# Split weights kept in one region of four rows, with rows that advance by 64 bytes in the first block

## The chip, the cores and the metric

The kernel runs on one core of one Trainium2 chip. The metric is the time of one execution on the device in microseconds (us); lower is better.

## What is computed

Two blocks follow each other on 256 tokens of width 2048, all in float32. The first (16 meta tokens are put in front, so 272 columns) is a projection of the normed input, an attention with an indexer, a gated recurrence, sigmoid gates, a branch product and an output product. The second is a modulated projection, a neighbourhood attention, a Fourier mix, long convolutions, an output product and a gated feed-forward layer.

```python
def hybrid_layer(x, ...):                      # first block, 272 tokens
    h = rms_norm(x, norm_g)
    proj = h @ w_in                            # 2048 x 12368
    ...
    p = jnp.einsum('btnc,ncd->btnd', y, w_branch)
    g = jax.nn.sigmoid(gates.reshape(B, T, N_BRANCH, D))
    merged = jnp.sum(g * p, axis=2)
    return x + merged @ w_out
...
def second_block(x, c, ctx, ...):              # 256 tokens
    mod = (s_lat @ ada_w[l] + ada_b[l])[:, None, :]
    q, k, v, f, hy = split_projection(h @ w_in[l])
    ...
    x = x + g1 * (y @ w_out[l])
    x = x + g2 * conv_gated_mlp(modulate(rmsnorm(x, norm2_g[l]), sh2, sc2), *ffn)
    return rmsnorm(x, final_norm_g)
```

## The kernel before

Every weight matrix passes through the core once, in **chunks**. A chunk is four k tiles (rows of 128) by 256 output columns, 1024 float32 in each of the 128 partitions. Four chunks are a unit (256 output columns over the whole depth of 2048), and the units follow the list PHASES: in the first block FB, QB, IB, QI, K, KA, QA, VA, ZB, ZA, GA, GB (200 chunks), then E and F, and for the second block G, H, IH, IF, J, IQ, OA, OB, L, M0, M1; 668 chunks in all. START gives a phase's first chunk: IB 32, QI 48, K 64, QA 76, VA 92, ZB 100, E 196.

The product is made in float32r from a high and a low part of each operand. For chunk c ScalarE (ACT, `hi`) copies the loaded float32 chunk from a ring of four 1 MB buffers `raw` into a slot `whi`, VectorE (DVE, `lo`) writes the difference to a slot `wlo`, and TensorE (PE, `chunk`) does for each k tile six matmuls: high by high, low by high, high by low, each for two halves h of the output. In the phases of kinds Tall, Tx, K, BR, T and T8 the weights are the stationary operand (128 columns of a slot), and a row of an activation plane is the moving one: `phi` and `plo` in the first block (`r_hi` and `r_lo` in FB), `y`, `f`, `c`, `o`, `e` planes behind it. Tall and K read all 272 tokens, Tx reads 256 from token 16 on. In H and J (N2) and in M0 and M1 (DN) the activations are stationary and the weights move.

The sequencer engines run their lists in order. The list of each is written by slots: slot c of PE is chunk c and then what small products are due at c; slot c of ACT is `hi(c + 4)` and then its small work; slot c of DVE is `lo(c + 4)` and then its own. There are four slots of each part. `hi(c)` therefore waits until PE has done chunk c - 4 (semaphore `mm` at c - 3). Three chunks of E wait for chunk c - 3 as well, since from E on the slots lie 64 bytes further.

Where things lie (bytes in a partition): the slots follow each other from byte 34944, 4096 each, so k tile k4 of a slot is at 1024 * k4 in it; from E on all of it 64 further. `phi` begins 32768 behind the slots' start; its rows are 272 float32, 1088 bytes. The `f`, `y`, `c` and `o` planes have rows of 1024 bytes, `e` (the first six units of L) rows of 1056.

## Time and profile before

| | |
|---|---|
| median of 3 runs | 2171.58 us (2169.76 to 2172.3) |
| the profiled execution's span | 2171.5 us, first to last instruction |
| its own time outside the span | none is given apart; the span is 0.1 us below the median |
| PE, matmuls | busy 2132.8 us, 16496 records |
| DVE | busy 1464.8 us |
| ACT | busy 1037.6 us |
| granted TensorE clock, mean | 0.996 |
| DMA | 470.05 MB, mean 216 GB/s |

An engine's busy time is the union of its instructions' intervals. The mean of one matmul in a group is longer than its share of the busy time, since matmuls overlap in the pipeline: the pace is read from the distance of starts. A float32 instruction of the small products can leave two records.

### The profile page before, as it was taken

How to read it: one execution, taken by the hardware profiler on the slowest of the kernel's cores; microseconds unless marked ns; L12 is line 12 of the kernel's file. 1: busy time of each engine (PE TensorE's matmuls, PEld its weight loads, DVE VectorE, ACT ScalarE, POOL GpSimd, SP SyncE). 2: the span in 40 equal slices, each digit the busy share in tenths (PEclk: the TensorE clock that was granted, in tenths of full speed). 3: DMA queues.
4: the chain of work that ended last, by engine and by line, in shares of the span. 5: the costliest groups of instructions: out<-in, count | busy, mean ns of one | idle time of the engine just before them, and what ended most of it. 6: DMA issues, size and time to landing. Idle time of an engine off the chain costs nothing.

```text
span 2171.5 us, 38030 instructions
## 1 busy us (share of the span) xinstructions
PE 2132.8 (98%) x16496; PEld 1987.9 (92%) x16496; DVE 1464.8 (67%) x1850; ACT 1037.6 (48%) x1418; POOL 25.0 (1%) x47
## 2 busy tenths in 40 slices
PE   7999999999999999999999999999999999999998
PEld 7989999988999999998788999999999999988886
DVE  7666556666757698696665577789666665555665
ACT  6554334444454465454433455465444444444454
POOL 0000000110000000000000000000000000000000
PEclk9999999999999999999999999999999999999999
DMA  9765655775448878786565655766777775555553
GB/s 326 239 208 195 196 194 176 232 243 162 153 156 263 295 256 267 252 285 223 182 224 166 233 175 192 255 210 229 240 245 240 243 242 195 194 193 190 182 196 112
DMA packets 339156, 470.05 MB, mean 216 GB/s; under 512 B 14797, under 2 KB 312557, under 8 KB 326126
## 3 DMA queue, kind: packets, MB, share of 16 engines
q1 hardware_dynamic: 337838, 466.93, 64.5%
q8 instruction: 130, 2.13, 0.4%
q0 software_dynamic: 1152, 0.70, 0.1%
q14 instruction: 36, 0.29, 0.0%
HBM read 464.80 MB, written 2.10 MB: 215 GB/s over the span
## 4 chain that ended last, share of the span: by engine, by line
PE 91%; DVE 5%; ACT 2%; DMA 2%; issue 1%; SPq 0%; ACTq 0%; DVEq 0%
PE ps L1971 64%; PE ps L1982 11%; PE ps L1990 4%; DVE wlo L1191 2%; PE ps L2002 1%; PE ps L2060 1%; ACT whi L595 1%; DMA raw<-w_branch_dram 1%; PE ps L2321 1%; PE ps L2261 1%; PE ps L2223 1%; PE ps L2255 1%; DVE arena L1257 1%; DMA raw<-w_in_dram 1%; PE ps L1926 1%
## 5 line engine op out<-in xcount | busy, mean ns | idle before, releaser
L1191 DVE TENSOR_TENSOR wlo<-raw,whi 128x1024 fp32r<-128x1024 f32 (+1 forms) x668 | 814.6, 1221 | 661.7 <-ACT whi L595 658.5
L595 ACT ACTIVATE whi<-raw 128x1024 fp32r<-128x1024 f32 (+1 forms) x668 | 706.3, 1058 | 1065.2 <-PE ps L1971 860.5
L1971 PE MATMUL ps<-f_hi,whi 128*128 128x256 f32 x2112 | 422.0, 281 | 1.6 <-DVE f_lo L1835 1.6
L1971 PE MATMUL ps<-f_lo,whi 128*128 128x256 f32 x2112 | 413.8, 277 | 0.0
L1971 PE MATMUL ps<-f_hi,wlo 128*128 128x256 f32 x2112 | 413.5, 277 | 0.0
L1971 PEld LDWEIGHTS ps<-f_hi,whi 128*128 128x128 f32 x2112 | 320.7, 188 | 14.3 <-issue 11.8
L1971 PEld LDWEIGHTS ps<-f_hi,wlo 128*128 128x128 f32 x2112 | 319.9, 188 | 0.0
L1971 PEld LDWEIGHTS ps<-f_lo,whi 128*128 128x128 f32 x2112 | 319.9, 188 | 0.0
L1971 PE MATMUL ps<-phi,whi 128*128 128x256 f32 (+2 forms) x1440 | 300.7, 290 | 0.0
L1971 PE MATMUL ps<-plo,whi 128*128 128x256 f32 (+2 forms) x1440 | 288.4, 281 | 0.0
L1971 PE MATMUL ps<-phi,wlo 128*128 128x256 f32 (+2 forms) x1440 | 288.1, 281 | 0.0
L1971 PEld LDWEIGHTS ps<-phi,whi 128*128 128x128 f32 (+1 forms) x1440 | 219.7, 188 | 20.5 <-issue 18.2
L1971 PEld LDWEIGHTS ps<-phi,wlo 128*128 128x128 f32 (+1 forms) x1440 | 219.9, 187 | 0.5
L1971 PEld LDWEIGHTS ps<-plo,whi 128*128 128x128 f32 (+1 forms) x1440 | 219.4, 187 | 0.5
L1257 DVE SCALAR_TENSOR_TENSOR arena<-raw,cst,arena 128x1024 f32<-128x1024 f32 x120 | 153.5, 1279 | 2.8
L1982 PE MATMUL ps<-wlo,dhi 128*128 128x512 f32 x336 | 90.8, 392 | 0.0
L1982 PE MATMUL ps<-whi,dlo 128*128 128x512 f32 x336 | 90.6, 392 | 0.0
L1982 PE MATMUL ps<-whi,dhi 128*128 128x512 f32 x336 | 90.3, 391 | 0.0
L1982 PEld LDWEIGHTS ps<-whi,dlo 128*128 128x128 f32 x336 | 63.1, 188 | 14.1
L1982 PEld LDWEIGHTS ps<-whi,dhi 128*128 128x128 f32 x336 | 63.0, 188 | 13.8
L1982 PEld LDWEIGHTS ps<-wlo,dhi 128*128 128x128 f32 x336 | 63.1, 188 | 13.5
L1971 PE MATMUL ps<-y_hi,whi 128*128 128x256 f32 x256 | 50.9, 281 | 2.9 <-DVE wlo L1191 2.9
(380 smaller groups left out, 2595.1 us busy)
## 6 DMA issues: line engine op xcount, KB each, us to landing
raw<-w_in_dram SPq DMA_DIRECT2D x151, 1024.0 KB, 5.9
raw<-ada_w_dram SPq DMA_DIRECT2D x96, 1024.0 KB, 5.0
raw<-ffn_w_up_dram SPq DMA_DIRECT2D x88, 1024.0 KB, 5.0
raw<-ffn_w_down_dram SPq DMA_DIRECT2D x44, 1024.0 KB, 5.2
raw<-w_out_dram SPq DMA_DIRECT2D x32, 1024.0 KB, 5.7
raw<-w_branch_dram SPq DMA_DIRECT2D x16, 1024.0 KB, 6.1
arena<-xT_dram SPq DMA_DIRECT2D x4, 544.0 KB, 6.6
arena<-ctxT_dram SPq DMA_DIRECT2D x1, 2048.0 KB, 11.1
```

What stands on the lines that cost most here:

```text
L595: nc.scalar.activation(whi[slot_of(c)][:, 0:w], src, ACT.Copy).then_inc(S("split_hi"), 1)
L1191: v.tensor_tensor(wlo[slot_of(c)][:, 0:w], src, whi[slot_of(c)][:, 0:w].bitcast(F32), ALU.subtract).then_inc(S("split_lo"), 1)
L1257: t = v.scalar_tensor_tensor(total, x, by, R(ADA_SUM[n - 1][half], 1024), ALU.mult, ALU.add)
L1926: l = mm(ps[2 * t + nb][:, :], x[:, kd, 128 * t:128 * t + 128], wx[:, 512 * nb:512 * nb + 512], start=False, stop=last)
L1971: l = mm(ps[2 * p + h][0:m, b:b + tt.stop - tt.start], wx[:, k], x[:, xi, tt], start=first, stop=last)
L1982: l = mm(ps[(4 if name == "M0" else 0) + 2 * t + nb][:, :], x[:, kd, 128 * t:128 * t + 128], wx[:, 512 * nb:512 * nb + 512], start=first, ...
L1990: l = mm(ps[2 * p + t][:, 0:UC], x[:, kt, 128 * t:128 * t + 128], wx[:, k], start=first, stop=last)
L2002: l = mm(ps[7][32 * j:32 * j + 32, :], cst[:, n % 16, :], raw[e % RING][:, 512 * j:512 * j + 512], start=n % 16 == 0, stop=n % 16 == 15)
L2060: x = mm(ps[4 + g % 2][:, 128 * (h - h0):128 * (h - h0) + 128], kk, qq, start=True, stop=True)
L2223: l = mm(ps[4 + m % 2][:, :], kF[:, kt, 128 * m:128 * m + 128], hfil[:, kt + (2 if m >= 2 else 0), :], start=kt == 0, stop=kt == 1)
L2255: l = mm(ps[4 + 2 * m + b // 2][:, :], kF[:, kt, 128 * b:128 * b + 128], u_tok[:, kt, 0:512], start=kt == 0, stop=kt == 1)
L2261: l = mm(ps[4 + t][:, :], kG[:, k, 128 * t:128 * t + 128], Yt[:, k, :], start=k == 0, stop=k == 3)
```

## The change

The eight slots become one region of four rows, one for each k tile of a chunk. Each row holds the high parts of the four slots (256 float32 each) and then the low parts. There are three views of the region. `w_all` (IB, K, KA, VA) and `w_own` (FB, QB, QI, QA, ZB, ZA, GA, GB), 64 bytes further, have rows of 2064 float32, 8256 bytes, which is 8192 + 64; `w_even`, from E on, has rows of 8192 bytes and begins where `w_all` does. The region takes 64 float32 more than the slots did, and the 48 float32 of `gains` are put between it and `phi`, so that `phi` begins 33216 bytes behind the region's start; `small` shrinks from 128 to 120 and its parts are renumbered.

The chunks at which the view changes wait for chunk c - 3 where they waited for chunk c - 4: the first three of IB, QI, K, QA, VA and ZB, 18 chunks (`moved`), and those of E as before. The split's outputs are written as four pieces 8256 or 8192 bytes apart, a stationary operand is 128 columns of one row, and the moving operand of M0 and M1 is two pieces of 256 in place of 512 in one. The instructions of every engine and their order stay as they are.

```diff
-        whi = [sb(f"whi{i}", [128, CW], F32R) for i in range(4)]
-        wlo = [sb(f"wlo{i}", [128, CW], F32R) for i in range(4)]
-
-        whi += [at(f"whi{4 + i}", [128, CW], MEM + RING * RW + CW * i + 16, F32R) for i in range(4)]
-        wlo += [at(f"wlo{4 + i}", [128, CW], MEM + RING * RW + CW * (4 + i) + 16, F32R) for i in range(4)]
-
-        def slot_of(c):
-            return c % 4 + (4 if c >= START["E"] else 0)
+        wbase = top[0]
+        w_all = at("w_all", [128, 4, 2064], wbase, F32R)
+        w_own = at("w_own", [128, 4, 2064], wbase + 16, F32R)
+        w_even = at("w_even", [128, 4, 2048], wbase, F32R)
+        top[0] += 8256
+        gains = sb("gains", [128, 48])
+
+        def view_of(name):
+
+            if START[name] >= START["E"]:
+                return w_even
+            return w_all if name in ("IB", "K", "KA", "VA") else w_own
+
+        def weights(c, low):
+
+            s = 256 * (7 - c % 4 if low else c % 4)
+            return view_of(UNITS[CHUNK[c][0]][0])[:, :, s:s + 256]
...
-        small = sb("small", [128, 128])
+        small = sb("small", [128, 120])
         modL = sb("modL", [128, 96])
         modC = sb("modC", [128, 32])
-        gains = sb("gains", [128, 48])
...
-        rq, rqs = small[:, 108:124], small[:, 72:88]
-        shw = small[:, 124:126]
+        rq, rqs = small[:, 104:120], small[:, 72:88]
+        shw = small[:, 2:4]
...
+            names = [name for name, _, _ in PHASES]
+            moved = {START[b] + i for a, b in zip(names, names[1:]) if view_of(a) is not view_of(b) for i in range(3)}
...
-                    act.wait_ge(S("mm"), c - 2 if START["E"] <= c < START["E"] + 3 else c - 3)
-                nc.scalar.activation(whi[slot_of(c)][:, 0:w], src, ACT.Copy).then_inc(S("split_hi"), 1)
+                    act.wait_ge(S("mm"), c - 2 if c in moved else c - 3)
+                nc.scalar.activation(weights(c, False)[:, :, 0:w // 4], rx(src, 4), ACT.Copy).then_inc(S("split_hi"), 1)
...
-                v.tensor_tensor(wlo[slot_of(c)][:, 0:w], src, whi[slot_of(c)][:, 0:w].bitcast(F32), ALU.subtract).then_inc(S("split_lo"), 1)
+                n = w // 4
+                v.tensor_tensor(weights(c, True)[:, :, 0:n], rx(src, 4), weights(c, False)[:, :, 0:n].bitcast(F32), ALU.subtract)\
+                    .then_inc(S("split_lo"), 1)
...
-                                k = slice(n * k4 + 128 * h, n * k4 + 128 * h + m)
-                                l = mm(ps[2 * p + h][0:m, b:b + tt.stop - tt.start], wx[:, k], x[:, xi, tt], start=first, stop=last)
+                                l = mm(ps[2 * p + h][0:m, b:b + tt.stop - tt.start], wx[:, k4, 128 * h:128 * h + m], x[:, xi, tt], start=first, stop=last)
...
-                                       wx[:, 512 * nb:512 * nb + 512], start=first, stop=last)
+                                       wx[:, 2 * nb:2 * nb + 2, :], start=first, stop=last)
```

In the order of ACT's instructions around the first chunks of IB only the operand of the split changes; L824 is an exponential of the recurrence, L619 the evacuation of a unit of QB. Before:

```order
L595 ACTIVATE whi_55<-raw_49 128x1024 [waits mm,loaded0]
L824 ACT_TABLE_LOAD
L824 ACTIVATE arena<-arena 128x2048 [waits lv_diff]
L595 ACTIVATE whi_56<-raw_49 128x1024 [waits mm]
L619 ACTIVATE arena<-ps 128x256 [waits mm]
```

Now, with the `mm` of the first L609 one chunk further on:

```order
L609 ACTIVATE w_all<-raw_49 128x4x256 [waits mm,loaded0]
L838 ACT_TABLE_LOAD
L838 ACTIVATE arena<-arena 128x2048 [waits lv_diff]
L609 ACTIVATE w_all<-raw_49 128x4x256 [waits mm]
L633 ACTIVATE arena<-ps 128x256 [waits mm]
```

Nothing moved past anything else; what is queued behind the first split waits with it.

## Rows read from the trace of the kernel before

**Rows 1.** The page: busy time by engine; the chain that ended last, by engine.

```profile
PE 2132.8 (98%) x16496; PEld 1987.9 (92%) x16496; DVE 1464.8 (67%) x1850; ACT 1037.6 (48%) x1418; POOL 25.0 (1%) x47
...
PE 91%; DVE 5%; ACT 2%; DMA 2%; issue 1%; SPq 0%; ACTq 0%; DVEq 0%
```

**Rows 2.** The page's costliest groups: busy us, mean ns of one, idle before.

```profile
L1971 PE MATMUL ps<-f_hi,whi 128*128 128x256 f32 x2112 | 422.0, 281 | 1.6 <-DVE f_lo L1835 1.6
...
L1971 PE MATMUL ps<-phi,whi 128*128 128x256 f32 (+2 forms) x1440 | 300.7, 290 | 0.0
...
L1982 PE MATMUL ps<-whi,dhi 128*128 128x512 f32 x336 | 90.3, 391 | 0.0
```

**Rows 3.** Timeline of PE in E: start us, us, group of instructions.

```profile
722.11 0.39 PE L1971 MATMUL ps<-y_hi,whi 128*128 128x256 f32 x2
...
724.83 0.39 PE L1971 MATMUL ps<-y_hi,whi 128*128 128x256 f32 x2
```

**Rows 4.** Timeline of PE in GB, one chunk and the next one's start.

```profile
699.73 0.40 PE L1971 MATMUL ps<-phi,whi 128*128 128x256 f32 x2
...
701.14 0.40 PE L1971 MATMUL ps<-phi,whi 128*128 128x256 f32 x2
...
701.83 0.39 PE L1971 MATMUL ps<-phi,whi 128*128 128x256 f32 x2
...
702.54 0.28 PE L1971 MATMUL ps<-phi,whi 128*128 128x256 f32 x1
```

**Rows 5.** Timeline of PE in FB, one chunk and the next one's start.

```profile
57.37 0.41 PE L1971 MATMUL ps<-r_hi,whi 128*128 128x272 f32 x2
...
58.87 0.41 PE L1971 MATMUL ps<-r_hi,whi 128*128 128x272 f32 x2
...
59.61 0.42 PE L1971 MATMUL ps<-r_hi,whi 128*128 128x272 f32 x2
...
60.37 0.41 PE L1971 MATMUL ps<-r_hi,whi 128*128 128x272 f32 x2
```

**Rows 6.** Timeline of PE in IQ, one chunk and the next one's start.

```profile
1207.95 0.40 PE L1971 MATMUL ps<-f_hi,whi 128*128 128x256 f32 x2
...
1210.78 0.40 PE L1971 MATMUL ps<-f_hi,whi 128*128 128x256 f32 x2
```

**Rows 7.** Timeline of ACT ahead of the first matmul group of the recurrence.

```profile
113.63 1.07 ACT L595 ACTIVATE whi<-raw 128x1024 fp32r<-128x1024 f32 x1 [1.80 <-PE ps L1971]
...
116.01 1.91 ACT L824 ACTIVATE arena<-arena 128x2048 f32<-128x2048 f32 x1
117.83 1.04 ACT L595 ACTIVATE whi<-raw 128x1024 fp32r<-128x1024 f32 x1
118.77 0.64 ACT L619 ACTIVATE arena<-ps 128x256 f32<-128x256 f32 x2
120.63 1.06 ACT L595 ACTIVATE whi<-raw 128x1024 fp32r<-128x1024 f32 x1 [1.22 <-PE ps L1971]
```

**Rows 8.** Timeline of PE, the first matmul group of the recurrence.

```profile
129.45 1.16 PE L2060 MATMUL ps<-arena 128*128 128x128 f32 x8 [2.91 <-DVE arena L1453]
```

**Rows 9.** Timeline of ACT in slot 97, in VA.

```profile
388.91 1.06 ACT L595 ACTIVATE whi<-raw 128x1024 fp32r<-128x1024 f32 x1 [1.96 <-PE ps L1971]
389.88 0.25 ACT L778 ACTIVATE arena<-ps 16x128 f32<-16x128 f32 x1
390.03 0.36 ACT L779 ACTIVATE arena<-ps 128x256 f32<-128x256 f32 x1
390.30 0.42 ACT L852 ACTIVATE arena<-arena 128x272 f32<-128x272 f32 x1
```

**Rows 10.** Timeline of PE behind chunk 98, in VA.

```profile
392.05 0.62 PE L2109 MATMUL ps<-arena,mean 128*128 128x272 f32 x2
```

**Rows 11.** Groups of DVE between 100 and 300 us: busy us, mean ns.

```profile
L1191 DVE TENSOR_TENSOR wlo<-raw,whi 128x1024 fp32r<-128x1024 f32 x48 | 58.8, 1224 | 74.2 <-ACT whi L595 74.2
...
L1453 DVE TENSOR_TENSOR arena<-arena 128x1024 f32<-128x1024 f32 x7 | 8.5, 1219 | 0.0
```

More of the change, by code:

```diff
@@ L477, in _ @@
                                      (kz, A["k_z"]),
-                                     (small[0:64, 104:105], A["hy_b1_2"].rearrange("a q -> q a")),
-                                     (small[0:64, 105:106], A["hy_b2_2"].rearrange("a q -> q a")),
-                                     (small[0:64, 106:107], A["hy_freq_2"].rearrange("a q -> q a"))):
+                                     (small[0:64, 100:101], A["hy_b1_2"].rearrange("a q -> q a")),
+                                     (small[0:64, 101:102], A["hy_b2_2"].rearrange("a q -> q a")),
+                                     (small[0:64, 102:103], A["hy_freq_2"].rearrange("a q -> q a"))):
                         sp.dma_start(dst, src).then_inc(S("mlp_in"), 16)
@@ L1711, in filters @@
                         dve.wait_ge(S("fm_mm"), i + 1)
-                        chain(v.tensor_scalar(d, ps[4 + i][0:64, 0:256], small[0:64, 104 + i:105 + i], small[0:64, 106:107], ALU.add, ALU.mult))
+                        chain(v.tensor_scalar(d, ps[4 + i][0:64, 0:256], small[0:64, 100 + i:101 + i], small[0:64, 102:103], ALU.add, ALU.mult))
                         chain(v.tensor_scalar(n, d, 1 / (2 * np.pi), MAGIC, ALU.mult, ALU.add))
@@ L1922, in down_last @@
                 kd = 4 * (len(UNITS) % 2 ^ 1) + q
-                w = slot_of(CHUNKS - 4 + q)
-                for x, wx, last in ((dhi, whi[w], False), (dlo, whi[w], False), (dhi, wlo[w], q == 3)):
+                wh, wl = weights(CHUNKS - 4 + q, False), weights(CHUNKS - 4 + q, True)
+                for x, wx, last in ((dhi, wh, False), (dlo, wh, False), (dhi, wl, q == 3)):
                     for nb in range(2):
-                        l = mm(ps[2 * t + nb][:, :], x[:, kd, 128 * t:128 * t + 128], wx[:, 512 * nb:512 * nb + 512], start=False, stop=last)
+                        l = mm(ps[2 * t + nb][:, :], x[:, kd, 128 * t:128 * t + 128], wx[:, 2 * nb:2 * nb + 2, :], start=False, stop=last)
                 return l
@@ L1941, in chunk @@
                     pe.wait_ge(S(f"gemm_free{p}"), (u - p) // 2)
-                wh, wl = whi[slot_of(c)], wlo[slot_of(c)]
+                wh, wl = weights(c, False), weights(c, True)
                 xh, xl = {"E": (y_hi, y_lo), "G": (c_hi, c_lo), "H": (c_hi, c_lo)}.get(name, (phi, plo) if kind in ("Tall", "Tx", "K") else (f_hi, f_lo))
@@ L1953, in chunk @@
                     cc = {"Tall": slice(0, T), "Tx": slice(META, T), "K": slice(0, T)}.get(kind, slice(0, 258 if early else 256))
-                    n = 144 if kind == "K" else UC
                     b = 256 * (q // 2) if kind == "BR" else 0
@@ L1986, in chunk @@
                         kt = 4 * q + k4
-                        k = slice(UC * k4, UC * k4 + UC)
                         for x, wx, first, last in ((xh, wh, kt == 0, False), (xl, wh, False, False), (xh, wl, False, kt == KT - 1)):
                             for t in range(2):
-                                l = mm(ps[2 * p + t][:, 0:UC], x[:, kt, 128 * t:128 * t + 128], wx[:, k], start=first, stop=last)
+                                l = mm(ps[2 * p + t][:, 0:UC], x[:, kt, 128 * t:128 * t + 128], wx[:, k4, :], start=first, stop=last)
                 l.then_inc(S("mm"), 1)
```

## The prediction

> **What bounds the kernel now.** I read the page first. PE is busy for 98% of the span, DVE and ACT for 67% and 48%, and 91% of the chain that ended last lies on PE [rows 1]. So the time is PE's, and two things can change it: the pace of the matmuls, and stalls of PE where another engine is late. The costliest groups are those of the weights' product; none waits for more than 1.6 us in all [rows 2], so I went on to the pace, in the timeline.
>
> The mean of one matmul (281 to 290 ns) isn't the pace, since matmuls overlap. A chunk is 24 matmuls, and the distance from its first start to that of the next chunk is its price. In E it is 724.83 - 722.11 = 2.72 us, 113 ns a matmul [rows 3]. In GB, with the same 256 columns, 702.54 - 699.73 = 2.81 us, 117 ns [rows 4]. In FB, with 272 columns, 60.37 - 57.37 = 3.00 us, 125 ns [rows 5]. The granted clock is full in all three, and no wait stands in these rows. What differs is where the operands lie.
>
> **How they lie.** While PE streams the moving operand of one matmul, it loads the weights of the next. I take the distance from the weights of the next matmul to the moving operand, modulo 256 bytes; multiples of 256 (the halves h, the planes with rows of 1024, the chunk q of a unit, whose four plane rows advance by 4 * 64) drop out. In E, F, OB and the later L it is -64, that is 192, all the time: the slots lie 64 further there and everything else is a multiple of 256. In the first block the plane's row advances by 1088 bytes and the weights by 1024, so the distance is 64, 128, 192, 0 over the four k tiles of a chunk where 256 columns are read (first column 16, which is 64 bytes), and 0, 64, 128, 192 for IB, KA and VA. The chunk of GB shows it: its first two k tiles take 701.14 - 699.73 = 1.41 us, 0.705 each, the third, at 192, takes 0.69, and the fourth 0.71; in E every k tile takes 2.72 / 4 = 0.68 [rows 3, 4]. FB, which starts at 64 as well, has 0.75, 0.75, 0.74 and 0.76 [rows 5]. So the distance of 192 is the quickest, and even there the k tile isn't as quick as E's, since it comes out of one at another distance.
>
> But 192 isn't enough. IQ reads the same `f` planes at the same 192, and its chunk takes 1210.78 - 1207.95 = 2.83 us, 118 ns [rows 6]. So at a constant distance there are two paces, and a stretch keeps that in which it began.
>
> **The change, part by part.** (1) Distances. After the change `phi` is 33216 bytes behind the region, 192 modulo 256, and 64 + 64 cancel where `w_own` and a start at column 16 meet. FB's plane lies 109120 bytes behind `phi`, 64 modulo 256, which with 192 and less the 64 of `w_own` is again 192. Rows of weights and of planes both advance by 64. So five of the six matmuls of a k tile are at 192, throughout the first block. The sixth isn't: during it the weights of the next row are loaded, 64 further, while the moving row is still the old one, so that it stands at 128. From E on both shifted by amounts that leave 192 as it was: no change there, in distance.
>
> What is that worth? Bounds from rows. At best E's pace: 2.72 in place of 2.81 for each of the 144 chunks with 256 columns (QB, QI, QA, ZB, ZA 16 each, GA, GB 32 each), 13.0 us; for the 52 chunks with 272 (FB, IB 16 each, KA, VA 8 each, K 4) the same overhead over the columns, E's 113 ns scaled by 272/256 to 120 ns, 2.88 in place of 3.00, 6.2 us. Together 19 us. At worst IQ's pace: 0.02 more on 144 chunks, +2.9 us, and nothing on the others. I take neither end, as every k tile has its one matmul at 128 and so re-enters 192, which is what GB's third k tile does: 0.69 for each of the four, 2.76, 0.05 less than now. I count 0.04 a chunk, since a chunk that follows small products begins from yet another phase, as IQ's does: 144 * 0.04 = 5.8 us. For FB's kind 4 * 0.74 = 2.96, 0.04 * 52 = 2.1 us. Sum -7.9 us.
>
> (2) Waits. At six edges (IB, QI, K, QA, VA, ZB) three splits wait for one chunk more, 18 chunks. PE has the weights themselves early enough: at E's edge this wait exists, and PE goes through it without idling [rows 3]. The price is what stands behind the split, on ACT and DVE in order. Two places are tight.
>
> IB's edge: the split at 113.63 starts with the end of a chunk of QB; one chunk more (2.81) makes it 116.44. Behind it are a table load and the exponential, 116.01 - 113.63 = 2.38 later, the next split 1.82 after that, the evacuation 0.94 after that and 0.64 long: 116.44 + 2.38 + 1.82 + 0.94 + 0.64 = 122.22 for the third split, which now starts at 120.63 [rows 7]. All that follows, a second table load, a SiLU, a split and two DVE products, hangs on it up to the first matmul group of the recurrence, for which PE already waits 2.91 [rows 8]. So +1.6 us.
>
> ZB's edge: ACT's slot 97 is a split at 388.91, two copies and a square at 390.30, 1.39 later, 0.42 long [rows 9]. PE's norm product behind chunk 98 needs the square and starts at 392.05, when the chunk is through [rows 10]. The split now waits for that chunk's end: 392.1 + 1.39 + 0.42 = 393.9, so PE idles 1.9 us.
>
> At the four other edges what PE needs one slot later are short copies and masks. I take 0.3 each, 1.3 in all, an estimate; below is 0, above the larger of the two prices each, 7.6. Sum of (2): +4.8.
>
> (3) Shapes. DVE and ACT write four pieces. The nearest row is L1453, which writes runs with gaps: 1219 ns against the split's 1224 for as many elements [rows 11], so nothing; ACT and DVE have idle time besides. The moving operand of M0 and M1 is two pieces of 256. No row shows such an operand; now it is one of 512, in three groups of 336 matmuls [rows 2]. If the second piece cost as much as a step from E's pace to IQ's does for two matmuls of 256, 2 * (118 - 113) = 10 ns, it would be 1008 * 10 ns = 10.1 us; a gain is excluded, since the same columns are read. I take 0, nearer to the 3 ns by which L1453's gaps differ from the split's: the pieces lie a multiple of 256 apart, and nothing is loaded between them. `gains` and `small` only move.
>
> (4) Some of what the pace gains is lost again: PE waits 2.91 for ACT and DVE at the recurrence's start, and 1.9 at ZB's edge, whose chains begin two or three chunks before. That is about ten chunks of 0.04, 0.4 us; I count 0.6.
>
> Sum: -7.9 + 4.8 + 0.6 = -2.5. The profiled execution's span is 2171.5, and the median of the runs is 2171.58, so no correction: **2169.0 us**. What this measurement can tell from no change is 0.2%, 4.3 us.
>
> [...]
>
> **The rivals.**
> (A) The forecast: pace between, waits as priced. 2164 to 2173. Chance 0.42.
> (B) The quick pace locks in, as in E, in spite of the sixth matmul. For it: E enters 192 out of GB's drifting distances and is quick from its first chunk. Against it: GB's third k tile. -19.2 + 4.8, and some 2 us lost at the waits: 2159; with 256 columns alone quick, 2165. Chance 0.24. It ends under 2165.
> (C) The change doesn't do what it is built on: not the distance sets the pace (the other engines' writes do, or the two paces of IQ and F are chosen by something else), or the first block falls into IQ's pace. 2171.5 + 4.8 = 2176.3, with IQ's pace 2179. For it: 192 alone gave IQ nothing. Chance 0.22, slower. It decides once the pace gains less than 0.5 us in all, which is 3 ns a chunk over the 196.
> (D) The split moving operand of M0 and M1 costs PE 4 to 10 ns each: +4 to +10 on the forecast, 2173 to 2179. Nothing shows it. Chance 0.12.
>
> **How the numbers follow.** The predicted time is (A)'s. (B) reaches down to 2159, (C) up to 2179; leaving out the outer part of both, 2160 to 2178. Faster by over 0.2% (below 2167.2): (B) and a quarter of (A), 0.35. Slower (above 2175.9): most of (C) and half of (D), and a little for edges dearer than priced, 0.28. Within: 0.37.
>
> **What would show it.** A chunk of GB at 2.76 or 2.77 (2.72 under (B), 2.81 or more under (C)), one of FB at 2.96. The wait of PE ahead of the recurrence near 4.5 in place of 2.91, and a new one of 1.9 at the norm product behind chunk 98. M0 and M1 as long as before, and E, F and L at 2.72. The prediction is wrong if the first block has one pace from the first to the last chunk (then the sixth matmul does nothing), or if a phase from IQ's to OA's changes its own between 2.72 and 2.83, as these stretches keep the pace with which they begin and 32 chunks of IQ are worth 3.5 us.

## The result, and the profile after

The changed kernel takes 2179.04 us, the median of 4 runs (2176.48 to 2182.19); the kernel before took 2171.94 beside it (4 runs, 2169.76 to 2172.36). The ratio is 1.0034, with a 95% interval of 1.0019 to 1.0050: 7 us slower. 2169.0 was forecast, with 2160 to 2178 as the range. The profiled execution has a span of 2177.5 us, 6.0 above that of before, and a granted clock of 0.994 in place of 0.996. In every run whose span is on record the time is 1.8 to 2.0 us above the span, so the profiled execution of before took about 2173.4 us (an estimate: 2171.5 and 1.9), 1.4 above its median of 2171.94; the profiled one of the changed kernel took 2179.41, 0.4 above its own.

The page of the changed kernel, its busy times, the chain by engine, and three of the costliest groups, which answer to [rows 1, 2]:

```profile
PE 2136.5 (98%) x16496; PEld 1990.9 (91%) x16496; DVE 1464.5 (67%) x1850; ACT 1035.9 (48%) x1418; POOL 25.0 (1%) x47
...
PE 90%; DVE 5%; ACT 2%; DMA 1%; issue 1%; SPq 0%; ACTq 0%; DVEq 0%
...
L1985 PE MATMUL ps<-f_hi,w_even 128*128 128x256 f32 x4224 | 674.0, 280 | 2.5 <-DVE f_lo L1851 2.5
...
L1985 PE MATMUL ps<-phi,w_own 128*128 128x256 f32 x2304 | 385.9, 284 | 0.0
...
L1996 PE MATMUL ps<-w_even,dhi 128*128 128x512 f32 x672 | 167.6, 392 | 0.0
```

High and low parts are now one tensor, so a group that reads both has twice the count. The shares are as they were; a difference of 0.3% must be looked for by place. The length of a phase is the time from its first matmul to that of the next, and its pace the mean distance of starts inside its chunks, both worked out from the trace's starts (distances that other work interrupts left out):

| phase | before, us | ns | after, us | ns | difference |
|---|---|---|---|---|---|
| FB, QB | 105.22 | 125.0, 117.2 | 105.21 | 124.6, 117.0 | -0.01 |
| IB | 68.73 | 125.3 | 73.06 | 124.5 | +4.33 |
| QI, K, KA | 109.46 | | 110.60 | | +1.14 |
| QA | 67.47 | 117.3 | 67.34 | 117.0 | -0.13 |
| VA | 33.92 | 125.1 | 37.56 | 124.5 | +3.64 |
| ZB, ZA, GA, GB | 322.53 | | 322.42 | | -0.11 |
| E, F | 182.95 | 113.4 | 183.24 | 114.5, 113.4 | +0.29 |
| G | 47.63 | 115.9 | 46.33 | 113.4 | -1.30 |
| H | 45.23 | 117.8 | 43.52 | 113.4 | -1.71 |
| IH to OB | 430.26 | | 430.29 | | +0.03 |
| L | 494.49 | 114.3 | 494.49 | 114.3 | 0.00 |
| M0, M1 | 241.48 | | 241.48 | | 0.00 |

The loss is in IB and VA, where the two tight waits are (at the recurrence, and at the norm product ahead of ZB's edge), and the hoped-for gain of pace isn't in the table. PE's timeline in GB, one chunk in k tiles (start us, us, group):

```profile
703.83 0.40 PE L1985 MATMUL ps<-plo,w_own 128*128 128x256 f32 x2
...
704.54 0.39 PE L1985 MATMUL ps<-plo,w_own 128*128 128x256 f32 x2
...
705.23 0.40 PE L1985 MATMUL ps<-plo,w_own 128*128 128x256 f32 x2
...
705.94 0.39 PE L1985 MATMUL ps<-plo,w_own 128*128 128x256 f32 x2
...
706.63 0.40 PE L1985 MATMUL ps<-plo,w_own 128*128 128x256 f32 x2
```

and in FB, likewise, one chunk:

```profile
56.85 0.41 PE L1985 MATMUL ps<-r_lo,w_own 128*128 128x272 f32 x2
...
59.84 0.41 PE L1985 MATMUL ps<-r_lo,w_own 128*128 128x272 f32 x2
```

GB's chunk takes 2.80 us where it took 2.81 [rows 4], FB's 2.99 where it took 3.00 [rows 5]; 2.77 and 2.96 were forecast. The k tiles of GB alternate between 0.71 and 0.69.

The two waits of PE are as forecast. Of ACT ahead of the recurrence, then in slot 97, which answer to [rows 7, 9]:

```profile
116.35 1.06 ACT L609 ACTIVATE w_all<-raw 128x1024 fp32r<-128x1024 f32 x1 [1.80 <-PE ps L1985]
...
122.02 1.06 ACT L609 ACTIVATE w_all<-raw 128x1024 fp32r<-128x1024 f32 x1
...
397.43 1.06 ACT L609 ACTIVATE w_own<-raw 128x1024 fp32r<-128x1024 f32 x1 [1.83 <-PE ps L1985]
...
398.81 0.41 ACT L866 ACTIVATE arena<-arena 128x272 f32<-128x272 f32 x1
```

and of PE, which answer to [rows 8, 10], with the matmuls behind them:

```profile
130.83 2.08 PE L2073 MATMUL ps<-arena 128*128 128x128 f32 x8 [4.41 <-DVE arena L1469]
...
133.16 0.66 PE L1985 MATMUL ps<-plo,w_all 128*128 128x272 f32 x2
...
134.52 0.66 PE L1985 MATMUL ps<-plo,w_all 128*128 128x272 f32 x2
...
399.27 1.10 PE L2122 MATMUL ps<-arena,mean 128*128 128x272 f32 x2 [1.89 <-ACT arena L866]
```

The first split stands at 116.35 (116.44 was worked out), the third at 122.02 (122.22), and PE waits 4.41 us in place of 2.91; at the norm product it waits 1.89 us, where it didn't wait. But these rows show more: behind the first wait six matmuls of 272 columns take 134.52 - 133.16 = 1.36 us, 227 ns each in place of 125, and the same eight small matmuls 2.08 us in place of 1.16. The granted clock was at half there: the trace's record of the clock has 0.5 for 6.83 us from 129.8 us on. The table of PE by stretches (window, its length and PE's busy time, granted clock, DMA share, GB/s) for the kernel before:

```profile
126.00:138.00 12.00, 9.09 (x73) 1.00 0.48 141
370.00:384.00 14.00, 14.00 (x102) 0.88 0.53 178
396.00:404.00 8.00, 8.00 (x70) 1.00 0.56 188
740.00:748.00 8.00, 5.08 (x35) 0.85 1.07 371
```

and for the changed one:

```profile
126.00:138.00 12.00, 7.59 (x40) 0.72 0.60 205
370.00:384.00 14.00, 14.00 (x109) 0.94 0.78 260
396.00:404.00 8.00, 6.12 (x35) 0.79 0.40 120
```

At the recurrence and at the norm product the full clock has become 0.72 and 0.79. In 126 to 138 the fall counts (1.00 - 0.72) * 12 = 3.4 us of work at full speed, in 396 to 404 it counts (1.00 - 0.79) * 8 = 1.7. By the same record such a fall is a stretch of 3.41 us at half, so each counts 1.7 at most; behind the first wait two follow each other. No step of the prediction has this.

### The profile page after: what moved, and what is told of

The parts are those of the page before. It is cut to its first block, busy times and chain, and to the rows that moved or that the text cites. A ratio compares the mean times of both kernels' runs of the same rounds, so it can differ in the third digit from the quotient of the medians.

```text
span 2177.5 us, 38030 instructions
## 1 busy us (share of the span) xinstructions
PE 2136.5 (98%) x16496; PEld 1990.9 (91%) x16496; DVE 1464.5 (67%) x1850; ACT 1035.9 (48%) x1418; POOL 25.0 (1%) x47
## 4 chain that ended last, share of the span: by engine, by line
PE 90%; DVE 5%; ACT 2%; DMA 1%; issue 1%; SPq 0%; ACTq 0%; DVEq 0%
PE ps L1985 63%; PE ps L1996 11%; PE ps L2003 4%; DVE w_even L1206 2%; PE ps L2073 1%; PE ps L2015 1%; ACT w_even L609 1%; DMA raw<-w_branch_dram 1%; DVE arena L1273 1%; PE ps L2334 1%; PE ps L2274 1%; PE ps L2236 1%; PE ps L2268 1%; DMA raw<-w_in_dram 1%; PE ps L1942 1%
## 5 line engine op out<-in xcount | busy, mean ns | idle before, releaser
L1206 DVE TENSOR_TENSOR w_even<-raw,w_even 128x1024 fp32r<-128x1024 f32 x472 | 577.1, 1224 | 427.2 <-ACT w_even L609 424.5
L609 ACT ACTIVATE w_even<-raw 128x1024 fp32r<-128x1024 f32 x472 | 499.8, 1060 | 693.8 <-PE ps L1985 496.6
L1985 PE MATMUL ps<-f_hi,w_even 128*128 128x256 f32 x4224 | 674.0, 280 | 2.5 <-DVE f_lo L1851 2.5
L1985 PEld LDWEIGHTS ps<-f_hi,w_even 128*128 128x128 f32 x4224 | 567.4, 189 | 15.5 <-issue 10.9
L1985 PE MATMUL ps<-f_lo,w_even 128*128 128x256 f32 x2112 | 414.7, 278 | 0.0
L1985 PE MATMUL ps<-phi,w_own 128*128 128x256 f32 x2304 | 385.9, 284 | 0.0
L1985 PEld LDWEIGHTS ps<-phi,w_own 128*128 128x128 f32 x2304 | 316.6, 189 | 15.6 <-issue 14.8
L1985 PEld LDWEIGHTS ps<-f_lo,w_even 128*128 128x128 f32 x2112 | 320.0, 189 | 0.0
L1206 DVE TENSOR_TENSOR w_own<-raw,w_own 128x1024 fp32r<-128x1024 f32 x160 | 195.3, 1224 | 182.5 <-ACT w_own L609 181.7
L609 ACT ACTIVATE w_own<-raw 128x1024 fp32r<-128x1024 f32 x160 | 169.2, 1058 | 285.5 <-PE ps L1985 283.6
L1985 PE MATMUL ps<-plo,w_own 128*128 128x256 f32 x1152 | 228.5, 280 | 0.0
L609 ACT ACTIVATE w_all<-raw 128x1024 fp32r<-128x1024 f32 (+1 forms) x36 | 36.2, 1014 | 83.1 <-PE ps L1985 83.1
```

What stands on the lines that cost most here:

```text
L609: nc.scalar.activation(weights(c, False)[:, :, 0:w // 4], rx(src, 4), ACT.Copy).then_inc(S("split_hi"), 1)
L1206: v.tensor_tensor(weights(c, True)[:, :, 0:n], rx(src, 4), weights(c, False)[:, :, 0:n].bitcast(F32), ALU.subtract)\
L1985: l = mm(ps[2 * p + h][0:m, b:b + tt.stop - tt.start], wx[:, k4, 128 * h:128 * h + m], x[:, xi, tt], start=first, stop=last)
```

## The experiments

Theory 1: the loss is that of the six edges, idle time and half a clock behind it; and the distance of addresses does set the pace, but a row that advances with its planes keeps one matmul in six at another distance, and that is enough to hold the pace back. Against it stand that the layout itself costs, that the distance is of no account, and that the half clock has nothing to do with the waits. The kernel before ran beside all of them, with medians of 2171.54 to 2173.26.

**The waits alone.** The old slots, with the later wait at the six edges:

```diff
-                    act.wait_ge(S("mm"), c - 2 if START["E"] <= c < START["E"] + 3 else c - 3)
+                    act.wait_ge(S("mm"), c - 2 if any(START[b] <= c < START[b] + 3 for b in ('IB', 'QI', 'K', 'QA', 'VA', 'ZB', 'E')) else c - 3)
```

> The kernel before with its old slots, where the first three splits of IB, QI, K, QA, VA and ZB wait for one chunk more, as in the changed kernel. Theory 1, the waits and the lower clock behind the two stalls of PE made the loss: 1.6 us more of waiting at the recurrence's first group, 1.9 at VA's norm product, about 1.1 at the other edges, and 3.4 and 1.7 us for the clock at half behind them; 2179 to 2183. Theory 2, the new layout made the loss (strided writes of the splits, the two-piece operand, the pace): the waits alone cost the 4.8 us of the prediction or less, 2172 to 2177, with no stretch of lower clock behind them.

2180.27 us (8 runs), ratio 1.0033 (1.0022 to 1.0045), the same as the whole change. IB is 4.62 longer than before and VA 3.75, QI, K and KA 1.0 together. Its PE:

```profile
131.59 2.08 PE L2060 MATMUL ps<-arena 128*128 128x128 f32 x8 [4.38 <-DVE arena L1453]
...
400.36 1.13 PE L2109 MATMUL ps<-arena,mean 128*128 128x272 f32 x2 [1.89 <-ACT arena L852]
```

**The layout alone.** All of the first block through `w_own`, which needs no edge but E's; IB, K, KA and VA then stand at 128:

```diff
-            return w_all if name in ("IB", "K", "KA", "VA") else w_own
+            return w_own
```

> The changed kernel with w_own for all of the first block, so that no view changes before E and no split waits longer; IB, K, KA and VA are read at a distance of 128 instead of 192. Theory 1: the loss goes, and with 272 columns at 124.5 ns and G and H at whichever of the two paces they fall into it takes 2167 to 2173. Theory 2: it stays at 2177 to 2181.

2174.28 us (10 runs), ratio 1.0008 (0.9997 to 1.0018). IB is 70.51 and VA 34.08, so without the waits the loss is gone, and the new region, the four-piece writes and the two-piece operand cost nothing that these runs can measure: the interval reaches to 4 us, but in the profile L, M0 and M1 are as long as before to 0.02 us. IB, KA and VA at 128 run at 125.9 ns where the changed kernel has 124.5 and the drifting distance of before 125.2.

**The wait kept, PE kept busy.** 14 small matmuls whose result nobody reads, ahead of the wait at the recurrence; in the second kernel 7 more ahead of that at the norm product:

```diff
+                    if l == 0 and g == 0:
+                        for _ in range(14):
+                            mm(ps[4][:, 0:128], mean1[:, :], ident[:, :], start=True, stop=True)
...
-                    pe.wait_ge(S("nk_sq"), c + 1)
                     if c >= 1:
                         pe.wait_ge(S("nk_root"), c)
+                    if c == 3:
+                        for _ in range(7):
+                            mm(ps[4][:, 0:128], mean1[:, :], ident[:, :], start=True, stop=True)
+                    pe.wait_ge(S("nk_sq"), c + 1)
```

> The changed kernel with 14 extra products of 128x128 float32 on PE (into a bank that is written next; their result is not used) ahead of its wait for the recurrence's first group, so that PE is busy for about 3 of the 4.4 us. Theory 1, with the lower clock as a result of PE's idling: the granted clock stays at full behind it, and 3.4 us come back, 2174 to 2177. Rival: the clock falls anyway (it comes with time, not with idling), and the time stays at 2177 to 2181.

> The changed kernel, waits and all, with 14 small matmuls without use ahead of PE's wait at the start of the recurrence (as in the run before with these alone) and 7 more ahead of its new wait at the norm product behind chunk 98 in VA. Nothing of the reference is left out. Theory 1 (the added waits cost twice: as idle time, and because the granted clock halves behind them): at the norm product PE stays busy through the 1.9 us, the stretch of half clock at 396 is gone, and VA is 1.5 us shorter than in the run with the first filling alone for an equal number of such stretches around 375; the whole 1.5 to 2 us under that run, so about 2174 to 2175, a ratio of 1.001 to the kernel before, where the changed kernel has 1.0034. Rival (the stretches fall where they do for another reason, and filling one moves it to the next): the stretch of 396 stays or comes back within the next 30 us, and the whole stays at 2176 to 2179.

With the first filling: 2176.43 us (10 runs), ratio 1.0016 (1.0007 to 1.0026). With both: 2174.98 us (11 runs), 1.0017 (1.0007 to 1.0026). The second's PE at the norm product, and its stretches:

```profile
396.03 1.72 PE L2126 MATMUL ps<-ident,mean 128*128 128x128 f32 x14
398.08 0.72 PE L2128 MATMUL ps<-arena,mean 128*128 128x272 f32 x2 [0.33 <-ACT arena L866]
```

```profile
126.00:138.00 12.00, 10.72 (x90) 1.00 0.60 204
370.00:384.00 14.00, 14.00 (x92) 0.77 0.77 254
396.00:404.00 8.00, 7.67 (x62) 1.00 0.44 135
```

What each wait is for is as in the changed kernel (the norm product's two waits have changed places, so that the filling stands between them), and the norm product starts 2.3 us behind the last pair of its chunk in both; what differs is that PE has work. The clock is full at both places. IB falls from 73.06 to 70.39 with the first filling and stays (70.41); VA goes from 39.16 to 37.60 with the second. So the half clock at these two places hangs on PE's idling. Both predictions of Theory 1 hold for their places. But the second row, 370 to 384, also shows what I can't steer: a stretch of half clock that is in the kernel before too (0.88 in that window). No wait of PE stands ahead of it. What stands there, in the kernel before, is 3.6 us of matmuls of one column:

```profile
372.49 3.62 PE L2179 MATMUL ps<-mean,arena 128*128 128x1 f32 x32
```

So PE's idling is one thing that the half clock comes behind, and not the only one. In both filled kernels this stretch is twice as long and takes back 1.5 us in the profile. Of the four profiles of kernels with a filling (two more follow below) three have it twice as long; of the ten without, nine have it once and one not at all. Whether a filling brings that about isn't shown. The second filling is worth 1.56 us in VA, but against the kernel before beside them the two kernels have the same ratio, 1.0016 and 1.0017, so the times don't show it. That the fillings act rests on IB and VA in the profiles.

**What distance is worth.** Four kernels change the layout from E on, where the kernel before stands at 192 and the rows of weights and planes advance alike. The first three are the kernel before with its late slots moved (16 to 0, 32 and 48 float32: distances 0, 128 and 64); the fourth is the changed kernel with `w_all` from E on, so that the weights' rows advance by 64 and the planes' don't:

```diff
-        whi += [at(f"whi{4 + i}", [128, CW], MEM + RING * RW + CW * i + 16, F32R) for i in range(4)]
-        wlo += [at(f"wlo{4 + i}", [128, CW], MEM + RING * RW + CW * (4 + i) + 16, F32R) for i in range(4)]
+        whi += [at(f"whi{4 + i}", [128, CW], MEM + RING * RW + CW * i + 0, F32R) for i in range(4)]
+        wlo += [at(f"wlo{4 + i}", [128, CW], MEM + RING * RW + CW * (4 + i) + 0, F32R) for i in range(4)]
...
             if START[name] >= START["E"]:
-                return w_even
+                return w_all
```

> The kernel before with the slots from E on not moved by 64 bytes, so that the distance from the next weights to the moving rows is 0 instead of 192, constant, in all phases whose weights are stationary. Theory 1 (the distance sets the pace): a chunk of L takes clearly more than 2.72 us, about the 2.83 of the drifting kernels, some 20 us or more in all. Theory 2 (a constant distance is enough, whichever it is): 2.72 us stay, 2170 to 2176 in all.

> As late_0, with the slots moved by 128 bytes from E on: a constant distance of 128, which is that of the sixth matmul of each k tile in the changed kernel's first block. Theory 1: slower than 2.72 us a chunk in L, and if this distance is the worst, more than 2.83, so that one matmul in six at it costs what the other five gain. Theory 2: 2.72 us.

> The kernel before with the late slots (from E on) 128 bytes further, so that from E on the next weights stand at a constant distance of 64 modulo 256 from the moving operand, where the kernel before has 192, and earlier runs had 0 (120.0 ns a matmul in L) and 128 (118.9). Theory 1 (the distance sets a pace of its own at each of four values, and 192 alone is quick): L at 118 to 120 ns a matmul, L about 18 to 22 us longer than 494.5, E to L alike, the whole about 2205 to 2211. Rival (only the distances 0 and 128 are slow, and the pace before is that of every other place): L stays at 113.3, and the whole within 5 us of 2172. For M0 and M1, whose weights move and whose activations are loaded, the distance becomes 192 by Theory 1's reckoning, and their 241.5 us shift by a few us in either direction.

> The changed kernel with the rows of 8256 bytes (w_all) from E on too, over planes with rows of 1024 bytes, so that the distance there goes through 192, 128, 64, 0 in each chunk. If the distance sets the pace as before it seemed to in GB, a chunk of F and of L takes 2.80 to 2.83 us in place of 2.72, some 15 to 20 us in all over 300 chunks. If what matters is something else that first and second block differ in (the planes' rows of 1088 bytes, the other engines' work), it stays at 2.72.

One run each: 2210.90, 2206.34, 2185.44 and 2210.35 us, where the runs of the kernel before beside all experiments range from 2168.77 to 2178.09. PE's timeline for distance 0, one chunk of L, and then 16 matmuls of M0 and M1:

```profile
1604.51 0.40 PE L1971 MATMUL ps<-f_hi,whi 128*128 128x256 f32 x2
...
1607.39 0.40 PE L1971 MATMUL ps<-f_hi,whi 128*128 128x256 f32 x2
...
2049.64 1.07 PE L1982 MATMUL ps<-whi,dhi 128*128 128x512 f32 x4
...
2053.26 1.07 PE L1982 MATMUL ps<-whi,dlo 128*128 128x512 f32 x4
```

for distance 128:

```profile
1597.83 0.40 PE L1971 MATMUL ps<-f_hi,whi 128*128 128x256 f32 x2
...
1600.68 0.40 PE L1971 MATMUL ps<-f_hi,whi 128*128 128x256 f32 x2
```

for distance 64, in E and in L:

```profile
722.33 0.40 PE L1971 MATMUL ps<-y_hi,whi 128*128 128x256 f32 x2
...
725.16 0.40 PE L1971 MATMUL ps<-y_hi,whi 128*128 128x256 f32 x2
...
1585.46 0.39 PE L1971 MATMUL ps<-f_hi,whi 128*128 128x256 f32 x2
...
1588.18 0.39 PE L1971 MATMUL ps<-f_hi,whi 128*128 128x256 f32 x2
```

and of the kernel before, 16 matmuls of M0 and M1:

```profile
2049.94 1.08 PE L1982 MATMUL ps<-whi,dlo 128*128 128x512 f32 x4
...
2053.61 0.62 PE L1982 MATMUL ps<-wlo,dhi 128*128 128x512 f32 x2
```

| distance | ns a matmul (L) | a chunk, us | L against before, us |
|---|---|---|---|
| 192 (before) | 113.3 or 117.8 | 2.72 or 2.83 | 0 |
| 64 | 113.3 or 117.8 | 2.72 or 2.83 | +4.6 |
| 128 | 118.9 | 2.85 | +18.6 |
| 0 | 120.0 | 2.88 | +23.5 |
| 192, 128, 64, 0 in turn | 118.0 | 2.83 | +16.5 |

The distance sets the pace; that is settled by kernels that differ in one number. It isn't the address of the weights alone: from E on the changed kernel has them, modulo 256 bytes, where the kernel at distance 0 has them, with the planes 64 bytes lower, and its L takes 494.49 us where the other's takes 518.01. I had expected 64 to be slow: it is the equal of 192, and each of them has two paces. 128 has two as well: L runs at 118.9, the greater part of IQ at 120.0. In E and F the kernel at 64 is in the slow one and in L for the most part in the quick one, at the same addresses within each phase.

**One matmul in six.** The undisturbed part of L read with the changed kernel's first-block addresses: the activations of its later units are put into `phi` and `plo`, whose rows are 1088 bytes, and read through `w_own`. Second, the kernel before with only its low slots moved on by 64 bytes, so that two loads of six stand at 128 and nothing advances:

```diff
-            if START[name] >= START["E"]:
+            if START[name] >= START["E"] and name != "L":
                 return w_even
...
+                rows = name == "L" and not early
+                if rows:
+                    xh, xl = phi, plo
```

```diff
-        wlo += [at(f"wlo{4 + i}", [128, CW], MEM + RING * RW + CW * (4 + i) + 16, F32R) for i in range(4)]
+        wlo += [at(f"wlo{4 + i}", [128, CW], MEM + RING * RW + CW * (4 + i) + 32, F32R) for i in range(4)]
```

> The changed kernel where L from its seventh unit on keeps its activations in phi and plo (rows of 1088 bytes) and reads its weights through w_own (rows of 8256 bytes): the first block's new addresses, in a phase that is quick and undisturbed. If one matmul in six at 128 is what undoes the gain, L's chunks take 2.80 us as GB's do, some 12 us more in all over 152 chunks. If the first block is slow for another reason (the other engines' work there), L stays at 2.72 and the time at 2176 to 2182.

> The kernel before with only the late low slots (wlo) 64 bytes further; the high ones stay. From E on, of six matmuls of a k tile two have low weights loaded ahead of them at a distance of 128, the other four stand at 192, and no row of weights moves against a row of activations. Theory 1 (a minority of matmuls at 128 is enough to undo the quick pace, as one in six seems to in the changed kernel's first block and in the run that read L's activations from rows of 1088 bytes): L at 116 to 119 ns a matmul, 12 to 24 us longer than 494.5, the whole 2190 to 2208. Rival (each matmul pays for its own distance): two in six at 118.9 and four at 113.3, a mean of 115.2, L about 8 us longer, the whole about 2183. Second rival (the advance of the rows itself is what costs): L at 113.3 to 114, the whole within 4 us of 2172.

The activations' writes go to the new planes too. One run each, 2202.87 and 2191.78 us. PE's timeline in L, one chunk, for the first:

```profile
1596.58 0.40 PE L1988 MATMUL ps<-plo,w_own 128*128 128x256 f32 x2
...
1599.41 0.40 PE L1988 MATMUL ps<-plo,w_own 128*128 128x256 f32 x2
```

and for the second:

```profile
1590.87 0.39 PE L1971 MATMUL ps<-f_hi,whi 128*128 128x256 f32 x2
...
1593.67 0.39 PE L1971 MATMUL ps<-f_hi,whi 128*128 128x256 f32 x2
```

2.83 us (118 ns) and 2.80 (116.6 ns), where the same chunk is 2.72 in the kernel before: L is 18.9 and 11.5 us longer. Of the 18.9, 15.7 lie in the 152 chunks that the edit is for; 3.2 lie in the six units ahead of them, where the change of view makes an edge and PE idles 2.50 us. If each matmul paid for its own distance, one in six at 118.9 would give 114.2 and two in six 115.2. They give more, so a minority at 128 holds the others back. That these are only the slow pace of 192 come by chance is unlikely: in the kernel before, the changed one and six others that leave L at a constant 192, L takes 494.46 to 494.49 us.

The first block of the changed kernel runs at 117.0, not 118. But from its 128th chunk on L does the same at these addresses; a chunk at 1851 us:

```profile
1851.00 0.39 PE L1988 MATMUL ps<-plo,w_own 128*128 128x256 f32 x2
...
1853.81 0.39 PE L1988 MATMUL ps<-plo,w_own 128*128 128x256 f32 x2
```

It takes 2.81 us. Matmul by matmul, the mean distances of starts over the first k tile of such chunks are 118.3, 116.7, 115.8, 114.2, 113.3 and 117.4 ns in L (43 chunks), and 118.5, 115.9, 116.4, 114.3, 113.0 and 117.2 in GB of the changed kernel (28 chunks). And QI of the changed kernel has chunks at 118.0. So this pattern has two paces too, 117 and 118, and L in a quiet stretch repeats the first block's: it is the addresses that hold the first block back, and not the other engines' work there.

M0 and M1 of the first of these kernels hold something that the edit doesn't explain. Their addresses are those of the changed kernel, where 12 matmuls take 2061.51 - 2058.77 = 2.74 us, and here they take 2.80:

```profile
2060.52 1.10 PE L1999 MATMUL ps<-w_even,dlo 128*128 128x512 f32 x4
...
2063.32 1.10 PE L1999 MATMUL ps<-w_even,dlo 128*128 128x512 f32 x4
```

M0 and M1 together are 4.7 us longer, at unchanged addresses. So here too one distance has two paces.

**A better version.** The layout in one view, with filling: in the first kernel 12 matmuls at the recurrence, 7 and 10 ahead of waits in E and F, and 8 ahead of the sums in OB. In the second 12 and 8 at the first and the last of these places, and for M0 and M1, whose loaded activations stand at 64, a view that puts them at 0, which had made them 2.3 us shorter above (2053.26 - 2049.64 = 3.62 us for 16 matmuls, where the kernel before has 2053.61 - 2049.94 = 3.67):

```diff
+        w_down = at("w_down", [128, 4, 2048], wbase + 48, F32R)
...
+            if name in ("M0", "M1"):
+                return w_down
```

> one_view (the new layout without the six edges) with 12, 7, 10 and 8 products of 128x128 float32 whose result is not used, ahead of four waits of PE (the recurrence's first group, a split in E, the planes at F's fourth chunk, the sums at OB). With PE busy while it would wait, the three stretches at half the clock that one_view's trace has there (127, 820 and, in other kernels, 1401 us) don't come: 1.7 us each, 2167 to 2171 against before's 2172 to 2173. Rival: the clock falls elsewhere instead, as it did in VA with the first filling, and the time stays at one_view's 2172 to 2175.

> The changed kernel with one view of the weights in the whole first block (no added wait but E's), 12 small matmuls without use ahead of PE's wait at the start of the recurrence, 8 ahead of its wait at the sums of OA/OB, and for M0 and M1 a view 192 bytes further, so that their loaded activations stand at a distance of 0 as in the run that was 2.3 us shorter there. No part of the reference is left out; the small matmuls are added work whose result is overwritten. Theory 1 (distance sets the pace; the clock falls where PE idles): M0 and M1 2.3 us shorter than 241.5, IB 68.9 as with the filling, OB 1.5 shorter, F at its 92 us, since nothing is filled there; the whole 2166 to 2169, 0.998 of the kernel before. Rival (the gains are chance phases of the pace and one undoes the other): within 2 us of 2172, 1.000.

2170.28 us (12 runs), ratio 0.9990 (0.9981 to 0.9998), and 2169.60 us (12 runs), 0.9983 (0.9973 to 0.9994). M0 and M1 took 239.16 in place of 241.48, and OB 47.33 in place of 49.05, as expected; but the layout in one view has that 47.33 without any filling, since no half clock came there, so that OB's gain isn't the filling's alone. F didn't follow: I had put its 94 us in the first kernel down to the filling in F, but in the second it is at the same pace without it (116.9 ns in both), so that reading fell. The second version is 0.17% under the kernel before by the ratio, 1.9 us by the medians, and its interval lies below that of the same layout without filling and without M0's view (0.9997 to 1.0018). So it is filling and M0's view that bring it, and not the change; the two kernels of this section are not told apart.

## Why the prediction was wrong

**The distances, step (1): the mechanism right, its size wrong.** Counted 7.9 us of gain (for 196 chunks, which is what the first block has; the 200 named at the start is a slip); the phases from QB to GB are together 0.5 us shorter than in the kernel with the waits alone (IB 0.29, QA, VA, ZB and KA 0.1 each, QI 0.2 longer). The step that failed is the one that "every k tile has its one matmul at 128 and so re-enters 192, which is what GB's third k tile does: 0.69 for each of the four". The four k tiles take 0.71, 0.69, 0.71, 0.69. The 0.69 was one k tile of a pattern that repeats, not what 192 costs behind a 128. Rival (C)'s result came, though not for the reason that it gives: the distance does set the pace, and (C) was worded as if it didn't. That its 2176 to 2179 fits the measured time is luck in part: it has neither the 4.6 us of the clock nor the 3.0 that G and H gave. That the distance does set the pace is shown where it is held constant: at 0 and 128 L is 23.5 and 18.6 us longer.

The two premises of the distance stand in the trace of before. One is that the weights of the next matmul are loaded while one streams. PE and its loads in QB (start us, us, group):

```profile
99.98 0.39 PE L1971 MATMUL ps<-phi,wlo 128*128 128x256 f32 x2
100.10 0.30 PEld L1971 LDWEIGHTS ps<-phi,whi 128*128 128x128 f32 x2
100.21 0.39 PE L1971 MATMUL ps<-phi,whi 128*128 128x256 f32 x2
100.33 0.30 PEld L1971 LDWEIGHTS ps<-plo,whi 128*128 128x128 f32 x2
100.44 0.40 PE L1971 MATMUL ps<-plo,whi 128*128 128x256 f32 x2
```

The load for the pair at 100.21 starts at 100.10, together with the second matmul of the pair at 99.98. So it is throughout: 13443 matmuls of the weights' product start less than 160 ns behind another of it, and each of their loads starts 2 to 5 ns behind the start of that other one. The other premise is that multiples of 256 bytes drop out. In GB the plane's rows go on by 4352 bytes from one q of a unit to the next and the slots by 4096, so that the distance grows by 256, and the undisturbed chunks of all four q (seven of each) take 2.807 us. What ties the pace to the distance inside the engine no run shows.

**The waits, step (2): right.** IB's edge +1.6 forecast, 4.41 - 2.91 = 1.5 measured; ZB's edge 1.9 and 1.89; the four others 1.3, and with the waits alone QI, K and KA took 1.0 more and VA 0.3 more than its wait and its half clock (3.75 - 1.89 - 1.52).

**What was missing: the granted clock behind the waits.** This is the second step that failed: the sum ended a stall at the instruction that ended it, and put what comes behind it at nothing. Behind these waits the clock stands at half for a while: that is what the 3.4 us at the recurrence and the 1.7 at the norm product are. The trace of before held the warning: the clock of before is 0.85 between 740 and 748 us, behind PE's wait of 2.92 in E. That wait stands on its page, among the costliest groups, of which the prediction says that none waits for more than 1.6:

```profile
L1971 PE MATMUL ps<-y_hi,whi 128*128 128x256 f32 x256 | 50.9, 281 | 2.9 <-DVE wlo L1191 2.9
```

The price of a stretch is read from kernels that differ in nothing else at the place: IB is 70.30 us with 3.4 us of half clock in the runs at distances 0 and 64, and 68.73 in the profile of before, 1.57; VA is 32.40 without, in the run at distance 128, and 33.92 with, 1.52. With the added wait of 1.89 in place, too: in the kernel whose weights' rows advance from E on, which has the changed kernel's first block, no stretch came behind the norm product's wait, and VA is 36.00 in place of 37.56. These same rows limit the point: at an unchanged wait of 2.91 us the clock fell in four of five profiles of the old first block, and the profile of before is the one in which it didn't. So a part of IB's +4.33 was luck of that execution, and the typical price of the longer wait is 1.5 of idling and a further 1.6.

**The account.** Of profile against profile: waits 1.5 + 1.9 + 1.3 = 4.7; clock 3.1 at IB (two stretches of 1.57) and 1.5 at VA (two where there was one), 4.6; first-block pace -0.5; E and F +0.3; G and H -3.0. Together 6.1, and the spans differ by 6.0. The medians differ by 7.1, since the profiled execution of before was a slower one of its kind (1.4 above its median by the estimate above, against 0.4). Of the 10.0 us between forecast and median, 7.4 are the missing gain of pace, 4.6 the clock, and G and H hide 3.0; 1.1 is this difference between profiles and medians.

**(3) and (4).** Shapes at 0 were right: L, M0 and M1 are the same to 0.01 us, so rival (D) is out: their two-piece operand costs nothing, and DVE's split stays at 1224 ns [rows 11]. Step (4) lost 0.6 of a gain that wasn't there.

**Not forecast at all: E, G and H.** "No change there, in distance" was right and "E, F and L at 2.72" was not. E of the changed kernel begins slow and turns quick without a change of address (PE's timeline, one chunk each):

```profile
735.46 0.40 PE L1985 MATMUL ps<-y_lo,w_even 128*128 128x256 f32 x2
...
738.28 0.40 PE L1985 MATMUL ps<-y_lo,w_even 128*128 128x256 f32 x2
...
754.85 0.39 PE L1985 MATMUL ps<-y_lo,w_even 128*128 128x256 f32 x2
...
757.58 0.39 PE L1985 MATMUL ps<-y_lo,w_even 128*128 128x256 f32 x2
```

2.82 and then 2.73 us; between them PE waited 1.53 us. G and H took the quick pace and gave 3.0 us. That isn't the layout's doing: the kernel with both fillings has the same addresses, and its G and H are 47.57 and 45.23, as before. The prediction's "a stretch keeps that in which it began" holds between interruptions alone: in the nine profiles at a constant 192 or 64 from E on, every change between the two paces within a phase stands at an interruption, where other matmuls or a wait put two starts over 160 ns apart (some 280 places), and none inside an unbroken run of chunks. In the kernel before G changes in this way at its eighth chunk. Which pace follows an interruption stays open; I tried nothing that sets it.

## What to carry to other kernels

A wait put into a loaded PE costs its idle time and, for each stretch of half clock behind it, 1.5 us more (1.57 in IB, 1.52 in VA); such stretches stand behind 26 of the 39 waits of 1.75 us and more: price both. Where the wait can't go, small matmuls without use ahead of it took the stretch away at both places here (IB from 73.06 to 70.39 us, VA from 39.16 to 37.60); look at the whole trace behind them, since a stretch elsewhere can grow. Before a layout is changed for pace, find the pace of the exact mixture of distances that it makes, in a long undisturbed phase; an even mean over matmuls (114.2 ns, where L took 118), or one k tile out of a pattern (0.69 us, where GB's four take 0.70 on the mean), doesn't give it. Where a phase has two paces at one address (G and H took 92.9 us together or 89.9), a difference of a few us in it says nothing of the edit until a second kernel with the same addresses shows it too.

## What the runs showed of the hardware

- The pace of a float32r matmul of 256 columns depends on the distance, modulo 256 bytes, between the weights being loaded and the moving operand: 120.0 ns at 0, 118.9 (in L) or 120.0 (in IQ) at 128, and at 64 and 192 either 113.3 or 117.8. A step of 256 changes nothing: 2.807 us a chunk for each q of GB in the kernel before. Other distances than these four were held constant in no run. In nine profiles at a constant 192 or 64 it changed between the two only where other work or a wait came between the chunks.
- The load of a matmul's weights starts with the matmul ahead of it: 2 to 5 ns behind the start of that one, for all 13443 of the weights' product that follow another within 160 ns in the kernel before.
- With the roles exchanged (512 columns of weights moving, activations loaded) the order is another one: M0 and M1 took 239.16 us at 0 (two kernels), 245.17 at 128 and 246.17 at 192 (one each), and at 64 241.48 in seven profiles and 246.2 in one. Here 0 is the quickest; that 64 is quicker than 192 isn't shown. I have no explanation.
- The granted clock falls to half (0.5 in the trace's record) in stretches of 3.41 us, or two of them on end, 6.83; at the end of each profile a longer one begins, 2.6 to 4.8 us behind PE's last matmul. Of those ahead of it: in the fourteen profiles one or two stretches stand behind 26 of the 39 waits of PE of 1.75 us and more, behind all four of 4.4 us two, and behind none of the 19 waits of 1.42 to 1.70 us. In thirteen of the fourteen one also begins behind, or within, a group of 32 matmuls of one column (3.6 us at full clock), without a wait.
- A moving operand in two pieces of 256, 1024 bytes each and 8192 apart, and split writes in four pieces cost nothing here: M0 and M1 take 241.48 us with both operands, and DVE's split takes 1223 to 1224 ns, ACT's 1056 to 1060, where they took 1224 and 1060.
